# First layer of a fused transformer kernel: silu of the gate columns as an exponential and three VectorE operations, uneven chunks, later splits

## The reference

```python
q, kc, vc, ks, vs, kw, vw, gate, z = split(u @ w_in)      # z: 512 x 1024
o = gate_c * o_compressed + gate_s * o_selected + gate_w * o_window
o = o.reshape(b, s, NSA_WIDTH) * silu(z)                   # silu(z) = z / (1 + exp(-z))
y = o @ w_out
```

## Time and profile before

| | us |
|---|---|
| median of 3 runs | 1406.42 |
| lowest and highest run | 1405.38, 1410.33 |
| the profiled execution, its own time | 1407.09 |
| its span in the profile | 1405.3 |
| PE busy | 1340.7 (95%) |
| ACT busy | 748.3 (53%) |
| DVE busy | 658.6 (47%) |
| POOL busy | 760.5 (54%) |
| mean granted clock of PE over the span | 0.994 |

### The profile page before, as it was taken

One profiled execution on the slowest core, in us unless ns is written; L12 is line 12 of the kernel. 1 busy time (PEld: TensorE's weight loads), 2 busy tenths in 40 slices (PEclk: granted clock), 3 DMA queues, 4 the chain that ended last, 5 costly groups with the idle time before them and its releaser, 6 DMA issues.

```text
span 1405.3 us, 20958 instructions
## 1 busy us (share of the span) xinstructions
PE 1340.7 (95%) x7738; PEld 1095.5 (78%) x7738; DVE 658.6 (47%) x1617; ACT 748.3 (53%) x1576; POOL 760.5 (54%) x796
## 2 busy tenths in 40 slices
PE   6999989998999999999999999999999999999997
PEld 5878767776888787887788888778889887778885
DVE  4343456676351444554330011891463436887135
ACT  4253378878542465665442323893544355887252
POOL 4443256656744456665554425687555524586652
PEclk9999999999999999999999999999999999999999
DMA  6242001001424322221443223334316223002322
GB/s 234 90 151 90 30 31 61 31 29 64 149 91 150 132 79 76 90 76 61 150 180 120 90 98 111 130 112 165 105 62 229 108 89 72 2 16 102 139 90 60
DMA packets 28901, 138.66 MB, mean 99 GB/s; under 512 B 3584, under 2 KB 4096, under 8 KB 18048
## 3 DMA queue, kind: packets, MB, share of 16 engines
q1 hardware_dynamic: 15200, 98.05, 19.9%
q10 hardware_dynamic: 13600, 39.27, 8.0%
HBM read 127.86 MB, written 8.39 MB: 97 GB/s over the span
## 4 chain that ended last, share of the span: by engine, by line
PE 76%; DVE 7%; ACT 7%; POOL 4%; issue 2%; DMA 2%; SPq 0%; POOLq 0%; ACTq 0%; DVEq 0%
PE psum L524 47%; PE psum L558 9%; PE psum L1472 3%; PE psum L1429 3%; PE psum L1500 3%; PE psum L1520 3%; DVE w_free L1582 2%; PE psum L1078 2%; ACT w_free L964 2%; POOL w_lo L479 2%; PE psum L1052 2%; DMA w_raw<-in_weights 1%; PE psum L774 1%; PE psum L1485 1%; ACT x_r L1642 1%
## 5 line engine op out<-in xcount | busy, mean ns | idle before, releaser
L479 POOL TENSOR_TENSOR w_lo<-w_raw,w_hi 128x512 fp32r<-128x512 f32 (+2 forms) x163 | 389.8, 2405 | 279.8 <-ACT w_hi L468 270.1
L468 ACT ACTIVATE w_hi<-w_raw 128x2048 fp32r<-128x2048 f32 (+2 forms) x92 | 159.2, 1731 | 91.8 <-DMA w_raw<-in_weights 77.8
L524 PE MATMUL psum<-w_hi,split 128*128 128x512 f32 x608 | 195.1, 394 | 3.2 <-POOL w_lo L479 2.2
L524 PE MATMUL psum<-u_lo,w_hi 128*128 128x512 f32 (+1 forms) x428 | 169.2, 395 | 1.6 <-POOL w_lo L479 1.6
L524 PE MATMUL psum<-u_hi,w_lo 128*128 128x512 f32 (+1 forms) x428 | 166.8, 390 | 0.0
L524 PE MATMUL psum<-u_hi,w_hi 128*128 128x512 f32 (+1 forms) x428 | 166.8, 390 | 0.0
L964 ACT ACTIVATE w_free<-w_free,neg_max 128x512 f32<-128x512 f32 (+3 forms) x256 | 148.2, 584 | 10.0 <-DVE neg_max L1582 9.0
L524 PE MATMUL psum<-w_hi,u_lo 128*128 128x512 f32 (+2 forms) x352 | 134.2, 381 | 1.8 <-DVE u_lo L924 1.8
L524 PEld LDWEIGHTS psum<-w_hi,split 128*128 128x128 f32 x608 | 114.2, 188 | 27.5 <-POOL w_lo L479 3.0
L524 PE MATMUL psum<-w_hi,u_hi 128*128 128x512 f32 (+2 forms) x352 | 132.5, 377 | 0.0
L524 PE MATMUL psum<-w_lo,u_hi 128*128 128x512 f32 (+2 forms) x352 | 132.5, 376 | 0.0
(11 more groups left out here) (240 smaller groups left out, 2793.3 us busy)
## 6 DMA issues: line engine op xcount, KB each, us to landing
w_raw<-in_weights SPq DMA_DIRECT2D x83, 1024.0 KB, 4.8
x<-x_scratch ACTq DMA_DIRECT2D x12, 512.0 KB, 4.9
w_raw<-in_weights SPq DMA_DIRECT2D x10, 512.0 KB, 4.6
gain<-in_gains ACTq DMA_DIRECT2D x9, 512.0 KB, 5.2
gain<-in_strips ACTq DMA_DIRECT2D x16, 256.0 KB, 2.9
spare<-in_strips ACTq DMA_DIRECT2D x16, 256.0 KB, 2.8
x_scratch<-x ACTq DMA_DIRECT2D x8, 512.0 KB, 4.0
gain<-in_near ACTq DMA_DIRECT2D x8, 512.0 KB, 4.2
```

Source lines behind the costliest of these rows:

```text
L468: high = nc.scalar.activation(w_hi[b][:, c], w_raw[b][:, c], ACT.Copy)
L479: low = nc.gpsimd.tensor_tensor(w_lo[b][:, c], w_raw[b][:, c], w_hi[b][:, c].bitcast(F32), ALU.subtract)
L524: mm = nc.tensor.matmul(dst, lhs, rhs, start=(a == 0 and k == 0 and (wl, ul) == (0, 1)), stop=(a + 1 == u and k + 1 == nk and (wl, ul) == ...
```

## The change

Silu is no longer one ACTIVATE. ACT writes exp(-z) from PSUM into the tile's home (`z_exponential`, at the places where `z_take` stood on ACT) and raises the new semaphore `z_exp`. DVE then adds 1 to it, takes the reciprocal, both in place in SBUF, and multiplies z out of PSUM with it (`z_take`, now on DVE, each operation waiting for the one before); only the last one frees the bank. On DVE this stands behind `score(i)` of step `z_step(t) + 2`, and for tile 0 ahead of `compress_turned_low`. `z_round` gives the four rounds of a pair from round 4 on 3, 2, 2 and 1 chunks in place of 2, 2, 2, 2. The z halves of the tiles from 4 on are split two steps later on both engines, and POOL's parts of the output units three steps later (56 to 71). The semaphores of the mla flow's strips, which had no user, are dropped.

```diff
--- before.py
+++ after.py
@@ -197,7 +197,7 @@

         w_loaded = [sem(f"w_loaded{b}") for b in range(SLOTS + 1)]
         z_loaded, z_high, z_ready = [sem("z_loaded0"), sem("z_loaded1")], sem("z_high"), sem("z_ready")
-        z_done, z_taken = sem("z_done"), sem("z_taken")
+        z_done, z_exp, z_taken = sem("z_done"), sem("z_exp"), sem("z_taken")
         cmp1_low = sem("cmp1_low")
         w_high, w_ready = sem("w_high"), sem("w_ready")
         w_used = sem("w_used")
@@ -248,7 +248,7 @@
                 self.inv, self.p = sem(f"{name}_inv"), sem(f"{name}_p")
                 self.turned, self.high, self.low = sem(f"{name}_turned"), sem(f"{name}_high"), sem(f"{name}_low")
                 self.pv = sem(f"{name}_pv")
-                self.strip = [sem(f"{name}_strip0"), sem(f"{name}_strip1")]
+                self.strip = [sem(f"{name}_strip{p}") for p in range(0 if name == "mla" else 2)]

             def group(self, g):
                 return self.list[2 * self.branches * g][:2]
@@ -1406,7 +1406,10 @@

         def z_round(d):

-            return (Z_FIRST + Z_EARLY * d, Z_EARLY) if d < 2 else (Z_FIRST + 2 * Z_EARLY + 2 * (d - 2), 2)
+            if d < 4:
+                return (Z_FIRST + Z_EARLY * d, Z_EARLY) if d < 2 else (Z_FIRST + 2 * Z_EARLY + 2 * (d - 2), 2)
+            shares = (3, 2, 2, 1)
+            return KC * (d // 4 + 2) + sum(shares[:d % 4]), shares[d % 4]

         def z_home(u):
             if u % 4 == 0:
@@ -1450,12 +1453,26 @@
                 if t == KC - 1:
                     pool.sem_inc(w_ready, NSA_OUT - Z_UNIT)

-        def z_take(act, t):
+        def z_exponential(act, t):

             act.wait_ge(z_done, t + 1)
             if t >= 4:
                 act.wait_ge(nsa_flow.gated, 2 * (t - 3))
-            nc.scalar.activation(z_home(t), bank(Z_BANK), ACT.Silu).then_inc(z_taken, 1)
+            nc.scalar.activation(z_home(t), bank(Z_BANK), ACT.Exp, scale=-1.0).then_inc(z_exp, 1)
+
+        def z_take(dve, t):
+
+            z = z_home(t)
+            dve.wait_ge(z_exp, t + 1)
+            done("dve", nc.vector.tensor_scalar(z, z, 1.0, None, ALU.add))
+            settle("dve", dve)
+            done("dve", nc.vector.reciprocal(z, z))
+            settle("dve", dve)
+            nc.vector.tensor_tensor(z, bank(Z_BANK), z, ALU.mult).then_inc(z_taken, 1)
+
+        def z_half_step(t):
+
+            return KC * (t - 2) - 4 if t > 2 else 1

         def pair_tensor(pe, f):

@@ -1621,6 +1638,10 @@
                     inverse(i - 2)
                 if i < f.steps:
                     score(i)
+                if f is nsa_flow:
+                    for t in range(1, KC):
+                        if i == z_step(t) + 2:
+                            z_take(dve, t)
                 if f is mla_flow and i == 0:
                     rope_add(dve, 2)
                     rope_add(dve, 3)
@@ -1659,9 +1680,9 @@
                         compress_turned_high(act, 3)
                     for t in range(1, KC):
                         if i == z_step(t) + 2:
-                            z_take(act, t)
+                            z_exponential(act, t)
                     for t in range(2, KC):
-                        if i == (z_step(t - 2) + 3 if t > 2 else 1):
+                        if i == z_half_step(t):
                             z_high_part(act, t)
                     if 51 <= i < 59:
                         split_high(act, NSA_OUT + (i - 51) // 4, (i - 51) % 4, 4)
@@ -1745,10 +1766,10 @@
                     normalise(f.steps - 1)
                 if f is nsa_flow:
                     for t in range(3, KC):
-                        if i - z_step(t - 2) - 4 in (0, 1):
-                            z_low_part(pool, t, i - z_step(t - 2) - 4)
-                    if 53 <= i < 69:
-                        split_low(pool, NSA_OUT + (i - 53) // 8, (i - 53) % 8, 8)
+                        if i - z_half_step(t) - 1 in (0, 1):
+                            z_low_part(pool, t, i - z_half_step(t) - 1)
+                    if 56 <= i < 72:
+                        split_low(pool, NSA_OUT + (i - 56) // 8, (i - 56) % 8, 8)
                 if f is mla_flow and 16 <= i < 24:
                     split_low(pool, RUNS["mla_out"]["unit"], i - 16, 8)
                 if f is mla_flow and i == f.steps + LAG + 2:
@@ -2554,7 +2575,7 @@
             for j in range(NT):
                 act.wait_ge(bank_done, 4 * RUNS["nsa_k"]["block"] + j + 1)
                 nc.scalar.activation(split[:, KH + j * T:KH + (j + 1) * T], bank(j), ACT.Copy).then_inc(split_hi, 1)
-            z_take(act, 0)
+            z_exponential(act, 0)
             for g in range(3):
                 compress_turned_high(act, g)
             pair_scalar(act, nsa_flow)
@@ -2685,6 +2706,7 @@
             compress_softmax_vector(dve, 0)
             compress_softmax_vector(dve, 1)
             project_vector(dve, "nsa_k", low_keys)
+            z_take(dve, 0)
             for g in range(3):
                 compress_turned_low(dve, g)
             pair_vector(dve, nsa_flow)
```

## The result

The changed kernel takes 1443.4 us (median of 4 runs, 1442.4 to 1445.3) against 1406.7 of the kernel before; the ratio is 1.026, 95% interval 1.024 to 1.028. The profiled execution took 1443.5 us, with a span of 1441.6, so 36.3 us more than the span of before. One execution told of further down, of the kernel with tanh and the take ahead of the scores, took 1882.8 us at a granted clock of 0.65 over its whole span, and is left out of that kernel's median.

The account below looks back on a forecast made before the run. PE, busy for 95% of the span, was taken as the bound, so gains could come only from its idle or half-clock time. 23.5 + 6.6 + 4.7 + 2.0 = +36.8; 1407.1 + 36.8 - 0.7 = 1443 us, range 1424 to 1456.

Parts of the forecast that it names:

- The reciprocal: In DVE's take, at 512 elements per row: 3.5 us, from the slope between the operation's rows at 2 and 32 elements.
- the rates that would have put it at 4.3 or 5.7 us: Reciprocal in DVE's take: 8.3 ns per element from the skill's repeat count of 8, or 11.0 ns as upper end (chance 0.03).
- The whole take: On DVE, addition 0.6, reciprocal 3.5, product 0.7 and gaps 0.1: 4.9 us, during which PE waits at the chunks.
- Tile 0: PE begins tile 1 at 170.0, 4.6 us later, and the clock falls over the idle time, +2.0: +6.6 us.
- Tile 1: PE starts at 180.3 instead of 176.39, +3.9, and the clock, which fell there before too, adds 0.8: +4.7 us.
- Five pairs: Takes 2 to 6, each with a waiting tile behind it: +4.7 us for each pair of rounds, +23.5 in all.
- PE's wait: At the first chunk of a pair (round 8), PE starts 4.6 us later because the bank is freed only after DVE's take.
- The clock: Behind PE's wait in every pair, PE's clock falls as after earlier idle times: 2.0 us each, between 1.6 and 2.5.
- Tile 7: No tile follows, but low(46) is queued behind the take on DVE and turn(47) waits for it: +2.0 us.
- Splits: z halves split two steps later, output parts three: 0; without cover 3 x 0.74 us at most, or as much the other way.
- the one on the chunks and the z split: Rounds of a pair: moving a chunk behind the wait counts 0; the z split on ACT, partly in the way, trims +4.9 to +4.7.
- The rival "faster": ACT's table loads bound round 8 and the take is nearly free, about 1.1 us: 1397 us, chance 0.04.

## Why the prediction was right

The time was forecast as 1443 and is 1443.4. By its own steps, with the terms read from the chains of both kernels:

- **The reciprocal:** 3.5 us, measured 3.35. Its slope between 2 and 32 elements held up to 512 within 5%, and the rates that would have put it at 4.3 or 5.7 us did not. The whole take was put at 4.9 us and measured 4.65.
- **Tile 0:** the chunks 4.6 later, measured 4.1 (169.58 against 165.44), and with the clock +6.6, measured +5.7 (scores at 174.15 against 168.44).
- **Tile 1:** +4.7, measured +4.6 (scores at 191.18 against 180.85, less the 5.7).
- **Five pairs:** +23.5, measured +24.0 (from those scores to the scores of round 24: 158.0 us, against 134.1 before; the rounds 2 and 3 in it are as long as before). The parts were right in kind and nearly in size. PE's wait grew by 4.2 us a pair (0.56 to 4.81), forecast 4.6. The clock cost 2.3 a pair, forecast 2.0: with PE kept busy the five pairs take 136.4 us against 147.7. And a pair with PE kept busy is 27.3 us, 2.4 over before with a wait 4.2 longer, so 1.8 of idle time went behind the wait, forecast 1.7.
- **Tile 7:** +2.0, measured +1.6 (9.4 us from the scores of round 24 to the turn, against 7.8), and PE then ran at half clock for less time than before, which gave back 1 us.
- **Splits:** 0; the last products with the values begin at 371.35 before and at 406.26 after, 34.9 later, which is the sum of the terms above, so the splits cost nothing up to there.
- **Behind the phase:** nothing was forecast, and 1.4 us came. 0.35 of it is a longer start ahead of one DVE operation (0.41 us against 0.06). The rest is a stretch of PE at half clock, where the same work before ran at full clock (windows of after, then of before):

```profile
508.30:511.60 3.30, 3.30 (x9) 2.58 (x8) 0.84 (x5) 2.61 (x5) 0.87 (x2) 0.50 0.47 199
```

```profile
473.40:480.00 6.60, 6.60 (x34) 5.15 (x34) 2.73 (x10) 4.64 (x10) 4.19 (x5) 1.00 0.18 74
```

Why the clock fell there, and whether the change has a part in it, stays open.

The mechanism was right: DVE's take ends last at PE's next chunk, its whole length is exposed, and the clock falls behind it. That the sum meets the median to 0.4 us is luck in part. The terms for tile 0 and the clock behind it were 0.9 too high, tile 7 was 1.4 too high, the five pairs 0.5 too low, and the 1.4 us behind the phase, which the sum did not have, made up most of the difference.

The step that was only half right is the one on the chunks and the z split. The sum left a possible gain from the split on ACT inside the rounding of 4.9 to 4.7, and said "the same work at both places: 0" of the chunks. With DVE's take in the way both are true (even chunks: 1442.5). Without it the two together gain 5.5 us, because rounds 8 and 9 then have idle time for a chunk and ACT's split stands in their chain.

The rival "faster" had put the point from which it decides at a take under 2.0 us. For the whole change this fits: with a take of 1.3 us the time is 1403.6, with one of 0.7 us 1396.3, against 1406.2 to 1406.6 before. But 5.5 us of that come from the chunks and splits. Against silu on ACT beside the same chunks and splits (1400.7), the take of 1.3 us is still 2.9 us slower and only the one of 0.7 us is faster: trading the table loads away pays here from somewhere between the two.

## What to carry to other kernels

Before a table load on ACT is traded for operations on another engine, price these at their real size. A reciprocal on DVE takes 6.5 ns for each element of a row (3353 ns by 512), where the addition and the product around it take 1.2 and 1.4, and two small rows of the trace were enough to see it. Ask then who stands behind the trade, and for how long: here one PSUM bank made an engine that was 95% busy wait for the whole length, and once the wait had grown from 0.6 to 4.8 us the clock fell too and took two fifths again (waits of 1.4 us, without the reciprocal, brought no fall in the five pairs; lengths between were not measured). And look for the formula that stays in the table that is loaded: tanh in the place of silu left one DVE operation of 0.69 us and won 1%. Before moving work between rounds, ask whether the round that it goes to has idle time: a chunk moved into such a round won its 0.7 us beside silu on ACT, and nothing where PE was busy or stopped by something else.

## What the runs showed of the hardware

A reciprocal of 128x512 took 3353 ns, each time, in place in SBUF; at 2 elements it took 159 and at 32 elements 353. TensorE's clock: PE idle for 4.8 us was followed by stretches of about 5 us at 0.50 to 0.66 of full clock in every pair, waits of 8.2 us lost no more than waits of 4.8, and with spare matmuls in the idle time the clock stayed at 1.00, so that 20 useless matmuls in each of five waits made a kernel 10.7 us faster. A switch to silu's table and back cost 2 x 1.28 us on ACT; the next ACTIVATE began within 0.02 us of the load's end, in all pairs.
